# Depthwise convolution of a conformer layer: five channel blocks on VectorE, three on TensorE

## The reference

```python
def conformer_conv(h, w_pw1, b_pw1, w_dw, b_dw, ln_g, ln_b, w_pw2, b_pw2):
    u = h @ w_pw1 + b_pw1                      # 256 x 1024 -> 256 x 2048
    a, g = jnp.split(u, 2, axis=-1)
    u = a * jax.nn.sigmoid(g)
    u = lax.conv_general_dilated(              # depthwise: 31 taps, each channel by itself
        u, w_dw[:, None, :].astype(u.dtype), window_strides=(1,),
        padding=[(CONV_WIDTH - 1, 0)],
        dimension_numbers=('NWC', 'WIO', 'NWC'),
        feature_group_count=D_MODEL) + b_dw
    u = jax.nn.silu(layer_norm(u, ln_g, ln_b))
    return u @ w_pw2 + b_pw2
```

## Time and profile before

| | us |
|---|---|
| median of 3 runs | 1726.85 |
| lowest, highest | 1724.46, 1729.49 |
| the profiled execution, its own time | 1730.17 |
| its span in the trace | 1728.4 |
| TensorE busy (matmuls) | 1549.5, 90% of the span |
| VectorE busy | 784.0, 45% |
| ScalarE busy | 690.1, 40% |

### The profile page before, as it was taken

One profiled execution on the slowest core, in us unless ns is written; L12 is line 12 of the kernel. 1 busy time (PEld: TensorE's weight loads), 2 busy tenths in 40 slices (PEclk: granted clock), 3 DMA queues, 4 the chain that ended last, 5 costly groups with the idle time before them and its releaser, 6 DMA issues.

```text
span 1728.4 us, 22658 instructions
## 1 busy us (share of the span) xinstructions
PE 1549.5 (90%) x8717; PEld 1182.8 (68%) x8717; DVE 784.0 (45%) x1039; ACT 690.1 (40%) x1017; POOL 9.2 (1%) x23
## 2 busy tenths in 40 slices
PE   6998999998999879877877878779999998999998
PEld 5866888887898656544544445446887886888876
DVE  5644654555759540100100001006998995554546
ACT  4544544444658420100100001005786873444435
POOL 1000000000000000000000000000000000000000
PEclk9966999999999869999999999999999998999999
DMA  9901555554540229999999999999999996556400
GB/s 323 337 30 50 188 193 194 182 187 160 161 156 13 73 74 387 386 387 387 387 387 387 387 387 387 387 387 386 386 387 387 387 387 215 192 178 195 146 1 25
DMA packets 221430, 442.16 MB, mean 256 GB/s; under 512 B 7059, under 2 KB 7398, under 8 KB 221366
## 3 DMA queue, kind: packets, MB, share of 16 engines
q1 hardware_dynamic: 220256, 438.46, 70.8%
q0 software_dynamic: 928, 2.79, 0.6%
q10 hardware_dynamic: 182, 0.05, 0.0%
HBM read 440.22 MB, written 1.05 MB: 255 GB/s over the span
## 4 chain that ended last, share of the span: by engine, by line
PE 72%; DMA 22%; DVE 3%; ACT 1%; issue 1%; SPq 1%; DVEq 0%; ACTq 0%
PE psum L440 18%; PE psum L441 17%; PE psum L442 17%; DMA weight_ring<-in_moe_w_gate 13%; DMA weight_ring<-in_moe_w_up 8%; PE psum L778 7%; PE psum L705 3%; PE psum L491 1%; PE psum L585 1%; PE psum L749 1%; PE psum L751 1%; PE psum L465 1%; PE psum L583 1%; SPq L335 1%; PE psum L833 1%
## 5 line engine op out<-in xcount | busy, mean ns | idle before, releaser
L1268 DVE TENSOR_TENSOR weight_lo<-weight_ring,weight_hi 128x1024 fp32r<-128x1024 f32 x412 | 498.2, 1223 | 279.2 <-ACT weight_hi L890 271.0
L890 ACT ACTIVATE weight_hi<-weight_ring 128x1024 fp32r<-128x1024 f32 x412 | 432.7, 1060 | 307.5 <-PE psum L442 306.6
L778 PE MATMUL psum<-weight_ring,silu_gate 128*64 128x256 f32 x2240 | 269.2, 386 | 65.9 <-DMA weight_ring<-in_moe_w_up 37.4
L440 PE MATMUL psum<-weight_hi,act_hi 128*128 128x512 f32 x672 | 267.9, 399 | 13.6 <-issue 5.6
L778 PEld LDWEIGHTS psum<-weight_ring,silu_gate 128*64 128x64 f32 x2240 | 156.8, 137 | 170.7 <-DMA weight_ring<-in_moe_w_up 60.3
L441 PE MATMUL psum<-weight_lo,act_hi 128*128 128x512 f32 x672 | 265.1, 394 | 0.0
L442 PE MATMUL psum<-weight_hi,act_lo 128*128 128x512 f32 x672 | 264.7, 394 | 0.0
L1765 DVE TENSOR_TENSOR hidden<-silu_gate,psum 128x256 f32<-128x256 f32 x35 | 14.7, 421 | 471.5 <-PE psum L778 471.5
L778 PE MATMUL psum<-weight_ring,hidden_T 128*64 128x256 f32 x1120 | 133.9, 383 | 38.2 <-DMA weight_ring<-in_moe_w_down 38.2
L1198 ACT ACTIVATE hidden_T<-psum 128x256 f32<-128x256 f32 x35 | 13.5, 385 | 374.6 <-PE psum L788 374.6
L440 PEld LDWEIGHTS psum<-weight_hi,act_hi 128*128 128x128 f32 x672 | 128.4, 191 | 41.3 <-issue 12.3
(11 more groups left out here) (281 smaller groups left out, 1480.1 us busy)
## 6 DMA issues: line engine op xcount, KB each, us to landing
weight_ring<-in_moe_w_gate SPq DMA_DIRECT2D x112, 1024.0 KB, 14.1
weight_ring<-in_moe_w_up SPq DMA_DIRECT2D x112, 1024.0 KB, 14.2
weight_ring<-in_moe_w_down SPq DMA_DIRECT2D x112, 1024.0 KB, 14.2
weight_ring<-in_ffn_w_gate SPq DMA_DIRECT2D x14, 1024.0 KB, 5.1
weight_ring<-in_ffn_w_up SPq DMA_DIRECT2D x14, 1024.0 KB, 5.1
weight_ring<-in_ffn_w_down SPq DMA_DIRECT2D x14, 1024.0 KB, 5.1
weight_ring<-in_attn_w_qkv SPq DMA_DIRECT2D x12, 1024.0 KB, 14.3
weight_ring<-in_conv_w_pw SPq DMA_DIRECT2D x12, 1024.0 KB, 5.0
```

The source lines that it names most:

```text
L440: pe.matmul(dst, ahi_, bhi_, start=first, stop=False, **kw)
L778: ins = pe.matmul(ps[rows, bank, 0:HW], lhs(k, half), raw(u)[:, cols], start=first and k == 0, stop=last and k == 1)
L890: act.activation(whi[:, u % SPLIT, :], raw(u), ACT.Copy).then_inc(hi_done, 1)
L1268: dve.tensor_tensor(wlo[:, u % SPLIT, :], raw(u), whi[:, u % SPLIT, :].bitcast(F32), ALU.subtract).then_inc(lo_done, 1)
```

## The change

The constants, TensorE's and ScalarE's part:

```diff
-PE_BLOCKS = [0, 1, 2, 3]
-DVE_BLOCKS = [4, 5, 6, 7]
+PE_BLOCKS = [5, 6, 7]
+DVE_BLOCKS = [0, 1, 2, 3, 4]
...
-            pe.wait_ge(glu_done, 1)
+            pe.wait_ge(glu_done, 2)
             for ch in PE_BLOCKS:
                 for k in range(TAPS):
                     pe.wait_ge(diag_done, n + 1)
-                    pe.matmul(ps[:, 4 + ch, 0:S], diag(n), cT[:, ch, k:k + S],
+                    pe.matmul(ps[:, ch, 0:S], diag(n), cT[:, ch, k:k + S],
                               start=k == 0, stop=k == TAPS - 1).then_inc(diag_used, 1)
                     n += 1
 
-            pe.wait_ge(glu_done, 2)
...
             split.to(U_PW1 + 7 + 4)
             sigmoids(0)
             diagonals(0, NDIAG)
             split.to(U_PW1 + 15 + 4)
-            diagonals(NDIAG, NDIAG + 4)
             sigmoids(1)
             split.to(U_PW2 + 4)
-            diagonals(NDIAG + 4, TAPS * len(PE_BLOCKS))
+            diagonals(NDIAG, TAPS * len(PE_BLOCKS))
             conv_out(len(PE_BLOCKS) - 1)
```

VectorE's part; `tap` is the old loop's body made a function:

```diff
+            EARLY = 8
             split.to(U_PW1 + 7 + 4)
             dve.wait_ge(rbc_done, 1)
             glu_scale(0)
             glu(0)
+            for k in range(EARLY):
+                split.to(U_PW1 + 8 + 4 + k)
+                for ch in DVE_BLOCKS[:4]:
+                    tap(k, ch)
             split.to(U_PW1 + 15 + 4)
             glu_scale(1)
             split.to(U_PW2 + 4)
             glu(1)
-
-            last_of = {}
-            for k in range(TAPS):
-                for ch in DVE_BLOCKS:
...
+            for k in range(EARLY):
+                tap(k, DVE_BLOCKS[4])
+                for ch in DVE_BLOCKS[:4]:
+                    tap(EARLY + k, ch)
+            for k in range(EARLY, TAPS - EARLY):
+                tap(k, DVE_BLOCKS[4])
+                for ch in DVE_BLOCKS[:4]:
+                    tap(EARLY + k, ch)
+            for k in range(TAPS - EARLY, TAPS):
+                tap(k, DVE_BLOCKS[4])
             dve.wait_ge(mean_done, 1)
```

More of the change, by code:

```diff
@@ L1134, in conv_out @@
                 act.wait_ge(diag_used, TAPS * (i + 1))
-                act.activation(cy[:, ch, :], ps[:, 4 + ch, 0:S], ACT.Identity,
+                act.activation(cy[:, ch, :], ps[:, ch, 0:S], ACT.Identity,
                                bias=vecs[:, V_BDW + ch:V_BDW + ch + 1]).then_inc(convp_done, 1)
@@ L1562, in glu, with tap @@
                 dve.sem_inc(glu_done, 1)
+            last_of = {}
+            def tap(k, ch):
+                src, w = cT[:, ch, k:k + S], taps[:, k * KT + ch:k * KT + ch + 1]
+                if k == 0:
+                    last_of[ch] = own.add(dve.tensor_scalar(
+                        cy[:, ch, :], src, w, vecs[:, V_BDW + ch:V_BDW + ch + 1], ALU.mult, ALU.add))
+                    return
+                own.wait(last_of[ch])
+                ins = dve.scalar_tensor_tensor(cy[:, ch, :], src, w, cy[:, ch, :], ALU.mult, ALU.add)
+                if k < TAPS - 1:
+                    last_of[ch] = own.add(ins)
+                else:
+                    ins.then_inc(conv_done, 1)
+            EARLY = 8
             split.to(U_PW1 + 7 + 4)
@@ L1571, in _ @@
             glu(1)
-            last_of = {}
-            for k in range(TAPS):
-                for ch in DVE_BLOCKS:
-                    src, w = cT[:, ch, k:k + S], taps[:, k * KT + ch:k * KT + ch + 1]
-                    if k == 0:
-                        last_of[ch] = own.add(dve.tensor_scalar(
-                            cy[:, ch, :], src, w, vecs[:, V_BDW + ch:V_BDW + ch + 1], ALU.mult, ALU.add))
-                        continue
-                    own.wait(last_of[ch])
-                    ins = dve.scalar_tensor_tensor(cy[:, ch, :], src, w, cy[:, ch, :], ALU.mult, ALU.add)
-                    if k < TAPS - 1:
-                        last_of[ch] = own.add(ins)
-                    else:
-                        ins.then_inc(conv_done, 1)
+            for k in range(EARLY):
[8 more added lines that the diff above has]
+                tap(k, DVE_BLOCKS[4])
             dve.wait_ge(mean_done, 1)
```

## The result

The changed kernel takes 1729.37 us (median of 22 runs, 1724.56 to 1730.86), the kernel before 1725.25 us in the same number of runs. The ratio is **1.0017, 95% interval 1.0010 to 1.0024**: slower by 2.9 us (1.7 to 4.1). The forecast was +1.7 us and no change within 0.3%. That held, and in the main so did the mechanism. Two terms were too small: the variance's, and what the early taps cost when TensorE comes back from its pause at full clock. One of the six executions of a later run, late8, took 5349.36 us where the other five took 1729.24 to 1732.05, and its ratio leaves that one out.

A forecast was written before the change was run, and what follows sets the result against it. The prediction took VectorE's last tap in the convolution stage as the bound. Its terms 0.22 - 0.18 + 0.83 + 0.43 + 0.4 = +1.7 us on the median 1726.85 gave 1728.5 us, range 1723 to 1735.

The forecast's parts named there:

- What bounds: Convolution stage: VectorE's last tap, 2.9 us behind TensorE's end, sets when the layer norm starts.
- Early taps in idle time: Between VectorE's splits: 32 taps fit into idle time; second `glu_scale` 1.00 us late, first tap behind the glu +0.22 us.
- The serial tail, +0.83: VectorE's last eight taps, all of block 4, each wait for the one before: +0.83 us, at most 1.95.
- VectorE's end at 566.8: End of VectorE's last tap: 565.92 + 0.22 - 0.18 + 0.83 = 566.8 us.
- TensorE hidden: TensorE's 93 taps, partly at half clock, end near 559.0, 7.8 us before VectorE: cost 0.
- The last mean matmul, +0.43: Layer norm's mean on TensorE: last matmul may take twice its 0.433 us at low clock, +0.43 us (0 to 0.43).
- The variance, +0.4: Layer norm's eight variance matmuls on TensorE: clock likelier low from the first on, +0.4 us (-1.9 to +1.5).
- The second projection and behind, 0: Second projection on TensorE: its half-clock spell may be shorter or longer, -1.6 to +1.6 us, taken as 0.
- The number: Whole kernel: median of the runs 1726.85 + 1.7 = 1728.5 us, no change within 0.3%; chance 0.58.
- the one that ends in a bound TensorE: Rival, convolution stage: over 18 of TensorE's 93 taps at half clock make it the bound, about 1758 us; chance 0.04.
- The one of early taps that don't fit: Rival, VectorE's splits: hand-overs without overlap make the second `glu_scale` some 0.9 us later still, 1729.4 us; chance 0.10.

The follow-up runs named there:

- late8: The kernel before with eight added VectorE additions, results unread, ahead of its last four taps; 1730.36 us, ratio 1.0033.
- split_block: The kernel before with its convolution redivided: TensorE does 18 taps of block 0 and blocks 1, 4, 5, VectorE the rest; 1718.80 us, ratio 0.9959.
- fill_gap: The changed kernel with 17 added unread matmuls ahead of TensorE's wait for the second glu; 1729.83 us, ratio 1.0026.
- the warm pair: Unread matmuls added in TensorE's layer-norm idle time: 16 in the kernel before, 1722.74 us; 22 in the changed kernel, 1725.77 us.
- spread: The changed kernel with block 4's taps spread among VectorE's others instead of eight in a row at the end; 1728.19 us, ratio 1.0011.
- no_early: The changed kernel with its 32 early taps moved behind the second glu; 1739.62 us, ratio 1.0075.
- late3: The kernel before with three added VectorE additions, results unread, ahead of its last four taps; 1728.46 us, ratio 1.0009.

## Why the prediction was right

- **What bounds.** VectorE's last tap, not TensorE as the chain named it. Right: TensorE was done with its taps 3.0 us sooner (559.82 instead of 562.87) and nothing behind it came sooner, and split_block, which took taps from both, gained 5.7 us at the mean copy.
- **Early taps in idle time.** Right in the first pair of profiles, not in the second. In the first: `glu_scale` at 510.41 (510.36 forecast), the first tap behind the glu at 517.30 (517.25), and without the early taps the end is 10.5 us later. There TensorE restarts at half clock, as in the rows of before. The step by which the lateness "is gone after four" splits took the due times of the splits from that one profile. Where TensorE restarts at full clock they are due 1.3 us sooner, the lateness is not worked off, and the first tap behind the glu is 1.16 us late instead of 0.22.
- **The serial tail, +0.83.** Right: 0.52 us apart, and 0.89 us gained without it. The Trainium skill's statement that a semaphore costs nothing extra (VectorE: DVE Perf Modes, "The DRAIN you can't avoid"), measured there on copies, doesn't carry over to these taps: one that waits for its direct predecessor starts 0.52 us behind it, others 0.396. The measurement decides.
- **VectorE's end at 566.8.** Right: 566.88.
- **TensorE hidden.** Right, with the size off by little: done at 559.8 instead of 559.0, since from 517 to 530 the clock was 0.81 on the mean, that is 4.9 us at half where I took 3. fill_gap shows that it costs nothing.
- **The last mean matmul, +0.43.** Right in the first profile and in fill_gap, but it was 0 in the changed kernel's second profile, where the mark is 0.52 us sooner.
- **The variance, +0.4.** The term that was mis-sized. It is +1.0 us in all three profiles with the tail of eight taps (root minus mean 9.18 to 9.27 against 8.22 and 8.23 before), and the warm pair shows it to be the clock. The clock was low from the first matmul on, as said, but the reason given, that TensorE does little from 559 on, doesn't hold: spread and no_early do as little, or less, and have 8.21 and 8.23. It came with the tail, which leaves one mean matmul alone at the end. That late3 and split_block ran the variance at full clock without added matmuls stays unexplained. So the tail cost 0.89 us on VectorE and brought up to 1.5 us on TensorE.
- **The second projection and behind, 0.** Open between bounds in the forecast, and open still. Counted from TensorE's restart, VectorE's later end is 0.9 us in the first pair of profiles and 1.9 in the second, the last mean matmul 0.4 and 0, the variance 1.0 in both: 2.4 and 2.7 us at the root (the parts are rounded). The loss of 2.9 us (1.7 to 4.1) holds both, so no rest is shown, and what the later stages add or give back isn't either.
- **The number.** That 1728.5 lies 0.9 us from the measured 1729.37 is in part luck. The three runs it started from had a median 1.6 us above that of the 22, and the difference of the kernels was 2.9 us where 1.7 was forecast.

Of the rivals, the one that ends in a bound TensorE needed 18 taps at half clock. (By the forecast's own numbers it is 21: at full clock TensorE ends at 557.5, 9.3 us before VectorE. The 7.8 us already hold the 1.5 at half clock.) It had 4.9 us at half clock, that is 5 or 6 taps. The one of early taps that don't fit fell in the first profile, with the row at 507.69, but its outcome came in the second: `glu_scale` starts 25.27 us behind TensorE's restart against 23.33 before, 1.9 us late, as 1.00 and its 0.9 make. The hand-overs weren't slower, as it had supposed; TensorE was faster.

## What to carry to other kernels

When two engines share a stage, compare their ends and not their shares of the chain: moving work off the engine that ends first gains nothing, and what counts is the work that both still have to do after the last input arrives. Share that in pieces smaller than the natural block if whole blocks leave one engine waiting. Don't let one accumulation's steps stand alone at the end of a queue, and count what a low clock costs the small matmuls on the path. An idle gap that is to be filled should be measured in several executions: here it was 1.3 us shorter when TensorE came back at full clock.

## What I hadn't expected of the hardware

- A delay of 2.68 us on VectorE cost 5.7 us (3.5 to 8.1) at the end, while behind one of 1.01 us the root came 0.66 us sooner in the one profile, the clock having held.
- Executions of one kernel differed by 5 to 9 us of 1725, with the DMA-bound 341.5 us the same to 0.01 us; the granted clock's spells at 0.50 were of other lengths in the two profiles of the kernel before.
- After the same 2.61 us of idling TensorE restarted at 0.50 in seven profiles and at 1.00 in six, with 1.34 us between them in the kernel before. After 7.90 us the restart at 0.50 cost 2.3 us (its taps took 42.56 us, with the gap filled 40.27).
